# Channel stage of a hybrid decoder layer: the two sums of pairs of squares are added on GpSimd before PE multiplies ones with them

## What is computed

```
def rmsnorm(x, g):
    xf = _f32(x)
    y = xf * lax.rsqrt(jnp.mean(xf * xf, axis=-1, keepdims=True) + NORM_EPS) * _f32(g)
    return y.astype(x.dtype)

def hybrid_layer(...):
    h = rmsnorm(x, norm_pre_mix)
    proj = _f32(h @ w_in)
    ...
```

## Time and profile before

| | us |
|---|---|
| median of 3 runs | 2903.26 |
| lowest and highest of the 3 | 2902.01, 2903.39 |
| span of the profiled execution (first to last instruction) | 2899.1 |
| PE busy in it | 2848.2 (98%) |
| DVE, ACT, POOL busy in it | 1904.1, 1191.8, 386.7 |
| mean granted TensorE clock, as a share of full speed | 0.994 |

### The profile page before, as it was taken

One profiled execution on the slowest core, in us unless ns is written; L12 is line 12 of the kernel. 1 busy time (PEld: TensorE's weight loads), 2 busy tenths in 40 slices (PEclk: granted clock), 3 DMA queues, 4 the chain that ended last, 5 costly groups with the idle time before them and its releaser, 6 DMA issues.

```text
span 2899.1 us, 36045 instructions
## 1 busy us (share of the span) xinstructions
PE 2848.2 (98%) x13576; PEld 2303.3 (79%) x13576; DVE 1904.1 (66%) x2616; ACT 1191.8 (41%) x2005; POOL 386.7 (13%) x496
## 2 busy tenths in 40 slices
PE   8999999999999999999999999999999999999998
PEld 5888887877777767888888788888788888888887
DVE  7677877666853358887343786666876555656656
ACT  6222222454443445545333533333533333545543
POOL 0000000012540236664121100000000000000000
PEclk9999999999999989999999999999999999999999
DMA  5222443446765958887878654444442223866862
GB/s 162 73 71 88 131 132 110 140 143 200 231 195 158 294 182 275 280 300 270 303 270 332 235 196 167 167 152 163 168 172 97 106 101 135 333 196 207 287 195 103
DMA packets 294569, 545.14 MB, mean 188 GB/s; under 512 B 59228, under 2 KB 150780, under 8 KB 284924
## 3 DMA queue, kind: packets, MB, share of 16 engines
q1 hardware_dynamic: 262636, 437.69, 45.2%
q0 software_dynamic: 24704, 75.52, 6.8%
q10 hardware_dynamic: 7056, 29.63, 2.6%
HBM read 358.30 MB, written 184.44 MB: 187 GB/s over the span
## 4 chain that ended last, share of the span: by engine, by line
PE 56%; DVE 3%; DMA 2%; ACT 1%; issue 1%; SPq 0%; ACTq 0%; DVEq 0%
PE f_banks L2985 25%; PE f_banks L2993 14%; PE f_banks L2087 7%; PE t_banks L1262 4%; PE t_side L1311 1%; PE t_banks L1278 1%; DMA f_h_raw<-hq 1%; PE t_side L1319 1%; PE t_side L1304 1%; PE t_side L1335 1%; DMA o_w_raw<-in_w_out 1%; PE t_side L1327 0%; PE f_banks L2290 0%; PE t_side L1342 0%; PE t_side L1292 0%
## 5 line engine op out<-in xcount | busy, mean ns | idle before, releaser
L2993 PE MATMUL f_banks<-f_d_op 128*128 128x512 f32 x1848 | 419.0, 389 | 0.0
L2993 PEld LDWEIGHTS f_banks<-f_d_op 128*128 128x128 f32 x1848 | 346.8, 188 | 72.0
L2832 DVE TENSOR_TENSOR f_d_op<-f_d_raw,f_d_op 128x1024 fp32r<-128x1024 f32 x154 | 187.6, 1225 | 148.8 <-ACT f_d_op L2663 148.2
L674 PE MATMUL t_banks<-h_hi,c_w_hi 128*128 128x512 f32 x640 | 254.5, 398 | 0.0
L1900 PE MATMUL t_banks<-t_w_hi,h_hi 128*128 128x512 f32 (+1 forms) x640 | 247.0, 386 | 5.0 <-DVE t_w_lo L1761 4.6
L674 PE MATMUL t_banks<-h_hi,c_w_lo 128*128 128x512 f32 x640 | 249.9, 390 | 0.0
L674 PE MATMUL t_banks<-h_lo,c_w_hi 128*128 128x512 f32 x640 | 249.1, 389 | 0.0
L2663 ACT ACTIVATE f_d_op<-f_d_raw 128x1024 fp32r<-128x1024 f32 x154 | 162.9, 1061 | 198.3 <-PE f_banks L2993 159.4
L1900 PE MATMUL t_banks<-t_w_lo,h_hi 128*128 128x512 f32 (+1 forms) x640 | 236.9, 370 | 0.0
L1900 PE MATMUL t_banks<-t_w_hi,h_lo 128*128 128x512 f32 (+1 forms) x640 | 236.1, 369 | 0.0
L2642 ACT ACTIVATE f_snap<-f_banks 128x1024 f32<-128x1024 f32 x88 | 90.3, 1026 | 253.6 <-PE f_banks L2985 253.6
(11 more groups left out here) (410 smaller groups left out, 6295.5 us busy)
## 6 DMA issues: line engine op xcount, KB each, us to landing
f_raw<-in_w_gu SPq DMA_DIRECT2D x88, 512.0 KB, 6.4
sop<-f_a SPq DMA_DIRECT2D x154, 256.0 KB, 2.0
f_d_raw<-sop SPq DMA_DIRECT2D x154, 256.0 KB, 3.0
t_raw<-in_w_tok SPq DMA_DIRECT2D x72, 512.0 KB, 4.6
f_d_raw<-top SPq DMA_DIRECT2D x88, 256.0 KB, 4.1
m_bc<-rows SPq DMA_DIRECT2D x16, 1152.0 KB, 6.8
f_d_raw<-in_w_dn SPq DMA_DIRECT2D x66, 256.0 KB, 3.6
o_y_lo<-y_lo SPq DMA_DIRECT2D x16, 1024.0 KB, 8.4
```

Of the source, the lines that this page charges most:

```text
L674: last = nc.tensor.matmul(banks[:, p % RING, :], w[:, n % 2, k, :], h[:, q, k, :], start=k == 0 and j == 0, stop=k == KD - 1 and j == 2)
L2832: tt(d_op[d % D_RING][:, 2:4], d_raw[:, d % S_RING], d_op[d % D_RING][:, 0:2].bitcast(F32), sub).then_inc(dlo_ok, 1)
L2993: last = nc.tensor.matmul(banks[:, bank, :], d_op[d % D_RING][:, s, tok], d_op[d % D_RING][:, w, :], start=k == 0 and j == 0, stop=k == FU ...
```

## The change

For blocks 1 to 3 a new list of GpSimd work, set ahead of its other work, waits until DVE has made both sums of pairs of a block (sqsum_ok), adds sq[2] onto sq[0] with one tensor_tensor of 128x1024, and signals a new semaphore sqall_ok. PE then waits for sqall_ok and multiplies ones with the two halves of sq[0] alone: two float32 matmuls for a block in place of four. Block 0 stays as it was. Each of the two matmuls now signals ones_mm, so that two signals for a block remain; ACT's squares for blocks 2 and 3 wait for both signals of the block before, where the first two of them waited for one. The semaphores wt_sent and ca_sent become one, parts_sent, which both stores of a round signal and which is waited for with twice the count.

```diff
+    def gpsimd(pool):
+        for q in range(1, BLK):
+            pool.wait_ge(sqsum_ok, 2 * q + 2)
+            nc.gpsimd.tensor_tensor(sq[0], sq[0], sq[2], ALU.add).then_inc(sqall_ok, 1)
+
@@ squares
-                act.wait_ge(ones_mm, 2 * (q - 1) + s // 2 + 1)
+                act.wait_ge(ones_mm, 2 * q if q >= 2 else s // 2 + 1)
@@ wt_out, and the same in the vector setup for ca_sent
-                act.wait_ge(wt_sent, 16 * e)
+                act.wait_ge(parts_sent, 32 * e)
@@ sums
+            if q:
+                pe.wait_ge(sqall_ok, q)
+                for k in range(2):
+                    nc.tensor.matmul(tr_banks[:, q % 2, :], ones[:], sq[0][:, k, :], start=k == 0, stop=k == 1).then_inc(ones_mm, 1)
+                return
             for pair in range(2):
-                pe.wait_ge(sqsum_ok, 2 * q + pair + 1)
+                pe.wait_ge(sqsum_ok, pair + 1)
                 for k in range(2):
-                    last = nc.tensor.matmul(tr_banks[:, q % 2, :], ones[:], sq[2 * pair][:, k, :],
+                    last = nc.tensor.matmul(tr_banks[:, 0, :], ones[:], sq[2 * pair][:, k, :],
                                             start=pair == 0 and k == 0, stop=pair == 1 and k == 1)
@@ gpsimd of the phase
+            c_gpsimd(pool)
             for unit in range(UNITS):
```

More of the change, by code:

```diff
@@ L176, in done @@
         return piece(n, BLK - 1) + 1
-    const_in, sqsum_ok, set_ok, act_chain, dve_chain = (
-        sem("c_" + s) for s in ("const_in", "sqsum_ok", "set_ok", "act_chain", "dve_chain"))
+    const_in, sqsum_ok, sqall_ok, set_ok, act_chain, dve_chain = (
+        sem("c_" + s) for s in ("const_in", "sqsum_ok", "sqall_ok", "set_ok", "act_chain", "dve_chain"))
     x_first = [sem("c_x_first%d" % i) for i in range(4)]
@@ L186, in channels @@
         sem("c_" + s) for s in ("w_ok", "wt_tr", "wt_ok", "ca_ok", "k_mm", "kern_ok", "tab_ok"))
-    wt_sent, ca_sent, kern_sent, tab_sent = (sem("c_" + s) for s in ("wt_sent", "ca_sent", "kern_sent", "tab_sent"))
+    parts_sent, kern_sent, tab_sent = (sem("c_" + s) for s in ("parts_sent", "kern_sent", "tab_sent"))
     sq_ok, ones_mm, rstd_ok, hraw_ok, hhi_ok, hlo_ok = (
@@ L221, in setup @@
             if s == 5 and e < EIGHTHS:
-                send_record(e, WT_AT, wt.rearrange("p (q m) -> p q m", q=2), wt_sent, wt_ok)
-                send_record(e, CA_AT, ca.rearrange("p q r m -> p q (r m)"), ca_sent, ca_ok)
+                send_record(e, WT_AT, wt.rearrange("p (q m) -> p q m", q=2), parts_sent, wt_ok)
+                send_record(e, CA_AT, ca.rearrange("p q r m -> p q (r m)"), parts_sent, ca_ok)
             elif s == 0 and e >= 1:
@@ L566, in setup @@
                         dve.wait_ge(k_mm, e)
-                        dve.wait_ge(ca_sent, 16 * e)
+                        dve.wait_ge(parts_sent, 32 * e)
                     product_re(o_re, pr, pi, xr, xi, t)
@@ L729, in setup_sent @@
         eng.wait_ge(kern_ok, EIGHTHS)
-        eng.wait_ge(wt_sent, 16 * EIGHTHS)
-        eng.wait_ge(ca_sent, 16 * EIGHTHS)
+        eng.wait_ge(parts_sent, 32 * EIGHTHS)
         eng.wait_ge(tab_sent, 16 * EIGHTHS)
@@ L769, in channels @@
                  banks_read)
-    return sync, scalar, vector, tensor, done_with
+    return sync, scalar, gpsimd, vector, tensor, done_with
 ROWS = 64
@@ L1434, in phase_tokens @@
         part_sent = sem("t_part_sent0"), sem("t_part_sent1")
-        c_sync, c_scalar, c_vector, c_tensor, done_with = channels(
+        c_sync, c_scalar, c_gpsimd, c_vector, c_tensor, done_with = channels(
             nc, sem, c_memory, banks, side[:, 0:2], side[:, 2], side[0:S5H, 3], *channel_inputs)
```

## The result

The changed kernel takes 2922.05 us (median of 4 runs, 2920.28 to 2923.51), the kernel before 2902.64 (4 runs). The medians lie 19.4 us apart; the ratio of the two kernels is 1.0064 with a 95% interval of 1.0052 to 1.0075, that is 18.6 us more, 15 to 22. A second series of both kernels gave 1.0071 (1.0055 to 1.0088), 20.6 us.

What follows compares the result with a forecast made beforehand. PE's work and a dependence ring were taken to bound blocks 1 to 3 equally. 3 x (2.20 + 2.35) + 3 x 1.6 = 18.5 us took the 2899.1 us span to 2917.6, plus 4.2 to the median: 2921.8, range 2911 to 2929.

Steps and rivals of the forecast that it cites:

- The two bounds: Blocks 1 to 3: PE's work (14.35 of 14.35 us a period) and a dependence ring of 14.37 us are equally late.
- PE's savings: Sums of blocks 1 to 3: four PE instructions a block go, 5.2 us in all, but 0 comes off the ring.
- The ring: Squares, sums, rstd, scaled x, next block's squares: grows 4.55 us a block, 2.20 waiting for DVE's lower_h plus 2.35 addition.
- The clock: After PE's idle wait in each of three blocks, sums and h_lo products run at lower clock: 1.6 us a block, 4.8.
- lower(1): DVE instruction in block 1, served after the addition, ending at 32.3 us before PE needs it at 34.8; costs nothing.
- the squares' waits: ACT's squares of blocks 2 and 3 wait for two signals, of sums already done; costs nothing.
- the merged semaphores: Record stores wait for both stores of a round, issued back to back half a round earlier; costs nothing.
- Does the delay stay?: After the sums of block 3: 0 of the delay expected to come back, at most 2 us.
- (a): Rival: GpSimd's addition doesn't wait for DVE; 7.4 to 12 us slower, 2911 to 2915; chance 0.12.
- (b): Rival: lock as forecast, but clock stays up or falls for little work; 13.7 to 15 us, 2917 to 2918; chance 0.15.
- (c): Rival: delay largely taken up again, or addition far quicker than the rows say; under 5.8 us left; chance 0.07.
- (d): Rival: PE's own work is the bound and the ring is not; 5.2 us gained, 2898.1; chance 0.03.

Runs made afterwards that it cites:

- e8: Changed kernel with GpSimd's list taken out and all additions on DVE in another order, two PE matmuls a block; 0.9996 of the kernel before, -1.2 us.
- e2: Changed kernel, but DVE waits for GpSimd's addition before it starts lower_h of the second half; 1.0048 of the kernel before, 13.9 us more.
- e4: Changed kernel with DVE waiting for the addition before lower_h and 14 needless products on PE ahead of its wait; 1.0025 of before, 7.3 us more.
- e3: Changed kernel with 24 needless products on PE ahead of its wait for GpSimd in blocks 1 to 3; 1.0034 of before, 9.9 us more.
- e10: Changed kernel with the change kept for block 1 alone; 1.0035 of before, 10.2 us more, 7.2 from the times of ACT's Ln.
- e1: Kernel before with only the merged semaphore and ACT's squares waiting for both signals, no change of arithmetic; 1.0001 of before.

## Why the prediction was right, point by point

**The two bounds, and nothing for PE's savings.** Shown by e8: PE's 12 instructions less, the ring about as it was (0.6 us longer), and no time that can be told.

**The ring grows by addition and wait.** Predicted 2.35 + 2.20 = 4.55 us a block. The addition measured 2.33 to 2.38 us where it ran alone (e2, e4), the wait 2.0 (e4 to e3; 1.6 from e2 to changed), with 0.1 us of hop in front. Signal, addition and wait sum to 4.4. This is the step on which the sign rested, and the two halves of it are shown apart. The Trainium skill's rule in "SBUF — State Buffer", section "SBUF: two separate sides", holds here in both directions: GpSimd's addition took 4.32 us behind lower_h, and lower(1) took 3.36 behind the addition.

**The clock.** Predicted 1.6 us a block from one row of before. Measured 1.6 (changed to e3, per block), 1.9 (e4 to e2), and 2.8 where it rose late (e10, 7.2 - 4.4, the next period included). One row of before had to stand for three blocks, and the clock did come back low in all three: 0.63, 0.62 and 0.62 over the sums. That is the pattern of the Trainium skill's section "HAM oscillation — how this bites in real kernels" in "TensorE: Matmul & The Clock Gate".

**lower(1), the squares' waits, the merged semaphores.** lower(1) took 3.36 us in place of 1.22 and ended at 33.02 us, and PE came to it later still, at 37.13; the rest is nothing (e1).

**Does the delay stay?** It did: from the Ln of block 3 to the first product of the token stage it is 476.7 us before and 476.8 changed. The step counted on 0 coming back and had no term for anything added later. In the traces the token stage of the changed kernel is 3.7 and 3.0 us longer than before, but the whole is only 0.7 and 1.1 us over the ring's part (18.6 and 20.6 against 17.9 and 19.5), so whether this kernel pays anything there is open.

**The number.** The sum of the ring, 18.5 against 17.9 us, is the part that was worked out. That 2921.8 agrees with 2922.05 to a quarter of a microsecond is luck. Two steps missed by 3 us each and cancel: the span was forecast at 2917.6 and is 2920.7 (ring 17.9, Ln of block 0 later by 1.05, token stage 3.7, the rest -1.1), and the distance from span to median was taken as 4.2, which is 1.4 now; in the runs on record the time lies 1.7 to 3.5 us above its own span, so a part of the 4.2 was a difference between single runs. The ring itself gave 17.9 us in one series and 19.5 in the other, the whole 18.6 (15.1 to 21.8) and 20.6 (16.0 to 25.6). The Ln times that the prediction named, "near 34, 54 and 75", are also 0.7 to 1.3 us below what its own sum gives (34.7, 55.3 and 75.8); measured were 35.5, 55.9 and 76.3.

**The rivals.** (a), no waiting for DVE, fell with the 4.32 us of the addition. (b), the clock without effect, fell with e3. (c), less than 5.8 us left, fell with the result, whose interval starts at 15. (d), PE's work as the bound, fell with e8.

## What to carry to other kernels

Before an operation is taken from the engine that is 98% busy, look for the ring of dependences in its stretch: if the ring is as long as the engine's work, what is taken away must also lie on the ring, and what is added to another engine must not. An addition moved to GpSimd beside a DVE that works on two SBUF inputs costs its own length and the length of whatever DVE has just begun. And a wait of PE that comes back every block has a second price in the clock behind it; filling the wait with useless products gave back 1.6 us of 6.

## What the runs showed of the hardware that I had not expected

- An addition of 8 columns on GpSimd was 2.11 us long behind a DVE operation of 2.28 us. So the duration that the trace shows has the wait in it.
- Additions on GpSimd in the first 75 us, even of 8 columns, were followed by a token stage of 524.6 to 528.2 us, against 521.6 to 524.4 without, in single traces. The whole times show it in four kernels and not in four others. The cause is open.
- How long the clock stays low after PE's wait varies between executions: in the changed kernel it rose within the last 0.6 us before the Ln in all three blocks in one series (17.9 us), and after it in the other (19.5 us; 0.50 from 52.5 to 57.0 us, with the Ln at 55.98); with block 1 alone changed it was at 0.50 of full speed over the sums and 0.71 over the 3.3 us after them.
